# A hybrid pooling, convolution and mixture-of-experts step: later state loads, a sample tile held in quarters, gathered rows used block by block, two added products

## The reference

```python
mod = silu(c) @ w_ada + b_ada              # 6 parts of 1024, a row per sequence
h = rmsnorm(x, norm1) * (1 + sc1) + sh1
u, gate_b, gate_c, val = split(h @ w_in)   # 4 x 512
pool_out, pool_state = pool_mixer(u, prefix, ...)      # trailing means over 2, 4, 8, 16 tokens
conv_out, conv_state = conv_mixer(gate_b, gate_c, val, ...)  # three taps over C*h
x = x + g1 * (concat([pool_out, conv_out]) @ w_out)
h2 = rmsnorm(x, norm2) * (1 + sc2) + sh2
logits = h2 @ w_router + b_router          # 32 experts, the best 4 of each token
x = x + g2 * moe(h2)                       # clamped SwiGLU, softmax over the 4 logits
y = rmsnorm(x, final_norm)
```

## Time and profile before

| | |
|---|---|
| median of 3 runs | 1306.57 us (1305.33 to 1307.25) |
| profiled execution, its own time | 1306.41 us |
| its span | 1304.6 us |
| PE busy | 1255.8 us, 96% of the span |
| DVE, ACT, POOL busy | 525.5, 90.9, 230.4 us |
| data moved | 487.32 MB, 374 GB/s over the span |
| start of the input projection | 41.84 us |
| start of the first expert's products | 278.74 us |
| idle time of PE from 290 us to the end of the experts | under 1 us |

### The profile page before, as it was taken

One profiled execution on the slowest core, in us unless ns is written; L12 is line 12 of the kernel. 1 busy time (PEld: TensorE's weight loads), 2 busy tenths in 40 slices (PEclk: granted clock), 3 DMA queues, 4 the chain that ended last, 5 costly groups with the idle time before them and its releaser, 6 DMA issues.

```text
span 1304.6 us, 32026 instructions
## 1 busy us (share of the span) xinstructions
PE 1255.8 (96%) x14083; PEld 578.7 (44%) x14083; DVE 525.5 (40%) x823; ACT 90.9 (7%) x166; POOL 230.4 (18%) x296
## 2 busy tenths in 40 slices
PE   3999999869999999999999999999999999999997
PEld 2687764523444444333333333333444444433344
DVE  1222313556444444444333333333444444444356
ACT  3210011210000000000000000000000000000002
POOL 5001200030111111122222211121111111112100
PEclk9899999969999999999999999999999999999999
DMA  9877762268999999999999999999999999999994
GB/s 323 278 278 279 274 261 94 104 260 347 408 424 424 426 426 425 425 426 420 421 427 424 423 429 416 425 426 424 425 423 417 427 428 424 427 427 425 423 422 156
DMA packets 63430, 487.32 MB, mean 374 GB/s; under 512 B 11191, under 2 KB 20759, under 8 KB 38053
## 3 DMA queue, kind: packets, MB, share of 16 engines
q1 hardware_dynamic: 47442, 455.92, 84.3%
q0 software_dynamic: 10592, 19.87, 4.2%
q10 hardware_dynamic: 5363, 11.05, 2.3%
HBM read 468.22 MB, written 25.88 MB: 379 GB/s over the span
## 4 chain that ended last, share of the span: by engine, by line
PE 93%; DVE 3%; DMA 2%; issue 1%; ACT 1%; SPq 0%; POOL 0%; DVEq 0%; POOLq 0%
PE acc L1943 51%; PE acc L1968 24%; PE acc L943 9%; PE acc L987 4%; DMA raw<-in_w_ada 2%; PE acc L860 1%; PE acc L2050 1%; PE acc L878 1%; PE acc L998 1%; ACT h_t L486 0%; PE acc L2066 0%; DVE picked L1624 0%; PE acc L959 0%; PE acc L983 0%; POOL rows L1412 0%
## 5 line engine op out<-in xcount | busy, mean ns | idle before, releaser
L1943 PE MATMUL acc<-raw_b,ht 128*32 128x512 f32 x3024 | 332.9, 596 | 5.7 <-DVE ht L1578 5.7
L1943 PE MATMUL acc<-raw,ht 128*32 128x512 f32 x2928 | 319.8, 592 | 0.0
L1681 DVE TENSOR_TENSOR g_sb<-acc,bias_gu 128x768 f32<-128x768 f32 x32 | 30.7, 958 | 521.9 <-PE acc L1943 521.9
L1412 POOL DMA_INDIRECT rows<-h_rows,row_next x90 | 92.7, 1030 | 701.3 <-DVE row_next L1573 654.1
L1943 PEld LDWEIGHTS acc<-raw_b,ht 128*32 128x32 f32 x3024 | 98.3, 111 | 234.7 <-issue 228.2
L1943 PEld LDWEIGHTS acc<-raw,ht 128*32 128x32 f32 x2928 | 95.1, 110 | 205.7 <-issue 200.4
L1968 PE MATMUL acc<-raw,at 128*32 128x256 f32 x2976 | 166.3, 379 | 0.0
L1968 PE MATMUL acc<-raw_b,at 128*32 128x256 f32 x2976 | 166.3, 379 | 0.0
L1968 PEld LDWEIGHTS acc<-raw_b,at 128*32 128x32 f32 x2976 | 96.7, 110 | 77.1 <-issue 18.5
L1968 PEld LDWEIGHTS acc<-raw,at 128*32 128x32 f32 x2976 | 96.7, 110 | 63.9
L943 PE MATMUL acc<-h_t,raw 128*128 128x288 f32 (+1 forms) x512 | 120.1, 397 | 1.1 <-DVE h_t L700 1.1
(11 more groups left out here) (257 smaller groups left out, 646.4 us busy)
## 6 DMA issues: line engine op xcount, KB each, us to landing
raw<-in_w_down SPq DMA_DIRECT2D x33, 2048.0 KB, 12.0
raw<-in_w_gate SPq DMA_DIRECT2D x31, 2048.0 KB, 9.1
raw<-in_w_up SPq DMA_DIRECT2D x31, 2048.0 KB, 13.4
raw_b<-in_w_gate SPq DMA_DIRECT2D x31, 2048.0 KB, 9.8
raw_b<-in_w_up SPq DMA_DIRECT2D x31, 2048.0 KB
raw_b<-in_w_down SPq DMA_DIRECT2D x31, 2048.0 KB
raw<-in_w_ada SPq DMA_DIRECT2D x24, 1024.0 KB, 11.7
expert_rows<-zeros ACTq DMA_DIRECT2D x1, 8704.0 KB, 30.6
```

What stands on the lines that cost most here:

```text
L1412: pool.indirect_dma_start(rows[:, b, :], None, h2_quarter, bass.IndirectOffsetOnAxis(ap=idx[:, b:b + 1], axis=0), bounds_check=Q * NTOK - ...
L1681: dve.tensor_tensor(g_sb[:, :, :], gate_of(i, 0), plus(0), ALU.add).then_inc(g_read, 1)
L1943: mm = pe.matmul(gu_of(i)[b][q * TB:(q + 1) * TB, :].rearrange("p (m n) -> p m n", m=2), ht_of(i)[:, b, k, :], w[:, kk, :, q * CW:(q + 1) ...
```

## The change

- **State loads.** In the opening ACT loads the bias rows of the parts sh1 and sc1 only. The loads of parameters and states, the bias rows of the other four parts, and four new loads of the sample rows (`x_q`) come after the modulation of `h_t`, ahead of the loads of L556 to L562. PE turns parameters and states between `project(2)` and `project(3)`; ACT copies them out (`empty_states`) after `leave(3)`, ahead of the issue of the zero fill and of `leave(4)`. DVE's pooling windows wait for that copy, as they did.
- **Sample tile in quarters.** `x_q` and `h_q` hold the sample rows as 4 x 32 partitions x 256 columns. A product with a constant `same_s` (built by POOL in five steps) adds the four partial sums of squares. The tile is turned by 2 transposes, not 8. ACT stores it as four transfers of 32 KB, and later copies `x_q` into `x_sb` for the final sum. The g1, shift and scale rows of the sample tile are read back as four transfers each, not one, on POOL's queue.
- **Order on PE.** The prompt state's transposes move behind the turning of tile 3 and write another PSUM pair; the sample states' transposes move behind the ranks and write `tp`; the g2 products wait until ACT has copied them out (`so_ready`, 4).
- **Rows block by block.** Expert 0's three gathers have a semaphore each. `turn_first` turns block after block, and `gate_up_first` multiplies each block by the first half of the weights' rows as it comes; the rest goes as before. The turning now stands ahead of the softmax sums on DVE. SP waits for the same three semaphores.
- **Two products** (`keep_clock`) of 128 x 512 on weights in slot 0 stand ahead of expert 0. Nothing reads their result.

```diff
+            ada_bias(SH1, SC1 + 1, rows_loaded)
             act.wait_ge(tp_full, TP["c"] + 1)
             act.activation(c_sg[:, :, :], c_ps, ACT.Sigmoid).then_inc(tp_free, 1)
             norm_row(n1_rows, norm1, rows_loaded)
-            act.dma_start(par_rows[0:GR, :], pool_scale[0].rearrange("(g p) -> g p", p=P)).then_inc(state_loaded, 16)
...
+            act.dma_start(sc_rows, state_conv[0].rearrange("b r d -> (b r) d")).then_inc(state_loaded, 16)
+            ada_bias(G1, PARTS, n2_loaded)
+            for q in range(Q):
+                act.dma_start(x_q[q * NS:(q + 1) * NS, :],
+                              x_sample.rearrange("b t d -> (b t) d")[:, q * QW:(q + 1) * QW]).then_inc(xq_loaded, 16)
             act.dma_start(wpool_sb[:, :, :], w_pool[0].rearrange("g c d -> c g d")).then_inc(small_loaded, 16)
...
             for g in range(GR):
                 leave(g, uext[:, g, PAST:PAST + SEQ], uext_s[:, g, :, PAST:PAST + DEC_T])
+                if g == GR - 1:
+                    empty_states()
...
+            dve.wait_ge(mix_done, TT)
+            dve.wait_ge(xq_loaded, 16 * Q)
+            step(dve.tensor_tensor(h_q[:, :], mixp[PT % 2][:, 0, 0:QW], g1_q[:, :], ALU.mult))
+            dve.tensor_tensor(x_q[:, :], x_q[:, :], h_q[:, :], ALU.add).then_inc(x1_ready, 1)
+            dve.wait_ge(x1_ready, TT)
+            step(dve.tensor_tensor(h_q[:, :], x_q[:, :], a2_q[0][:, :], ALU.mult))
+            best(PT - 2)
+            dve.wait_ge(sq_done, TT + 1)
+            step(dve.reciprocal(rstd_q[:, :], rstd_q[:, :]))
+            dve.scalar_tensor_tensor(out=h_q[:, :], in0=h_q[:, :], scalar=rstd_q[:, 0:1], in1=a2_q[1][:, :],
+                                     op0=ALU.mult, op1=ALU.add).then_inc(h_ready, 1)
...
-            for k in range(4):
+            for k in range(3):
                 project(k)
+            pe.wait_ge(state_loaded, 16 * 4)
+            take("par")
...
+            pe.matmul(ss_ps, same_s[:, :], ss_q[:, 0:1], start=True, stop=True).then_inc(ss_summed, 1)
+            router(3)
+            take("h4")
...
+                def turn_first():
+                    for b in range(SB):
+                        dve.wait_ge(first_gathered[b], 16)
+                        ins = dve.transpose(ht[:, b, :, :], rows[:, b, :].rearrange("p (i k) -> p k i", k=KT))
+                        ins.then_inc(first_turned, 1)
...
+                def keep_clock():
+
+                    pe.wait_ge(slot_loaded[0], loaded_value(0, 0))
+                    for n in range(2):
+                        pe.matmul(psum[:, 1, :], slots(0)[:, n * P:(n + 1) * P], slots(0)[:, HALF:2 * HALF],
+                                  start=True, stop=True)
...
+                pe.wait_ge(so_ready, 4)
...
-                gate_up(0)
+                keep_clock()
+                gate_up_first()
```

More of the change, by code:

```diff
@@ new lines, in _ @@
+            act.wait_ge(h_ready, TT + PT + 1)
+            for q in range(Q):
+                act.dma_start(h2_dram[SEQ:NTOK, q * QW:(q + 1) * QW], h_q[q * NS:(q + 1) * NS, :])\
+                    .then_inc(h2_stored[PT % 2], 16)
+            act.wait_ge(so0_full, 1)
+            states(0, acc_u)
+            for q in range(Q):
+                act.activation(x_sb[0:NS, PT, q * QW:(q + 1) * QW], x_q[q * NS:(q + 1) * NS, :], ACT.Copy)\
+                    .then_inc(xs_rows, 1)
+            act.wait_ge(so_full, 1)
```

242 lines of the change are left out of this document (134 added, 108 removed).

## The result

The changed kernel takes 1312.26 us (median of 6 runs, 1311.15 to 1313.25) beside 1306.86 us for the kernel before (6 runs, 1304.03 to 1307.34). The ratio is 1.0045, 95% interval 1.0032 to 1.0058. It is slower by 0.45%; 1302.5 was forecast. The profiled execution took 1311.15 us, with a span of 1309.4 us; before it was 1304.6.

The account below looks back on a forecast made before the run. PE, holding 93% of the chain of waits, was taken as the bound. Opening and projection +4.55 us (-2.4 - 1.95 + 3.6 + 1.5 + 3.8) and tail -8.6 gave -4.05: 1306.57 to 1302.5 us, range 1297.5 to 1307.5.

Parts of the forecast that it names:

- opening: traffic and transposes: Before the projection: less load traffic gains 2.4 us, and state transposes moved off PE's way gain 1.95 us.
- block 2 waits for ACT: First projection blocks: twelve added issues delay ACT's first copy, so block 2 waits; +3.6 us, bounds 1.7 and 5.6.
- lower clock in blocks 6 and 7: Projection after the parameters and states: a lower clock there only raised that term's upper bound, 4.8 instead of 3.8 us.
- tail, up to the end of the first expert's gate and up products: From mix(4): first expert starts 6.2 us earlier, regained clock gives 2.4; together -8.6 us, between -5.5 and -10.
- twelve take 5.8 us: ACT's queue ahead of its first projection copy: twelve added issues at 0.485 us each take 5.8 us.
- the stall of the `br_bc` issue grows with what lies ahead of it: ACT's queue in the projection: the 4.61 us stall grows by 2 us; used only for block 2's upper bound, 5.6.
- a first expert that starts d earlier should end the run d earlier: Expert loop: weights are there in time and PE hardly waits, so an earlier first expert shortens the run equally.
- the weights of the second expert are late: Expert loop: one of three listed signs that would show the prediction wrong; no size given.
- The slower one: Projection: ACT's issue queue fills, block 2 starts 26 us behind the projection's start; projection part +11.6, time 1309.6; chance 0.08.
- The one on the stores: Ahead of the gathers: last quarter store lands at 268 or later, gain 5.5 instead of 8.6, time 1305.6; chance 0.15.
- The rival that the clock does not come back: First expert: despite the two products the clock returns no earlier, 2.8 us lost as before, time 1304.9; chance 0.10.
- The fastest one, small stalls: Projection: short issues, clock stays up, traffic gain 3.5; projection part about 0, time 1298; chance 0.22.

Follow-up runs that it names:

- e12: e10 without the two products ahead of the first expert; 1297.80 us, ratio 0.9949 to the kernel before.
- e1: Changed kernel with opening and projection as before the change, only its tail (from mix(4) on) kept; 1302.29 us, ratio 0.9972 to the kernel before.
- e4: Changed kernel without the two products (`keep_clock`) ahead of the first expert; 1310.55 us, ratio 1.0038 to the kernel before.
- e6: Changed kernel, but SP issues the later slots' expert weights only after the four quarter stores have landed; 1313.19 us, ratio 1.0060 to the kernel before.
- e8: Changed kernel with the first expert's rows turned in one step when all three blocks have landed; 1313.19 us, ratio 1.0056 to the kernel before.
- e10: Changed kernel with the edits of e9, e3 and e7 together; 1296.25 us, ratio 0.9927 to the kernel before.
- e9: Changed kernel with all ACT issues but the four state loads moved behind the copies of the first two blocks; 1303.71 us, ratio 0.9984 to the kernel before.
- e5: Changed kernel plus unused 128 x 512 products, five ahead of block 2 and two ahead of block 6; 1305.57 us, ratio 0.9996 to the kernel before.
- e3: Changed kernel with ACT copying block 4 before parameters and states, not after; 1308.13 us, ratio 1.0020 to the kernel before.
- e7: Changed kernel, but weights of expert 1's second part are issued only when expert 1's rows have landed; 1307.87 us, ratio 1.0018 to the kernel before.
- e11: e1 with e7's wait for expert 1's rows ahead of the second part's weights; 1299.32 us, ratio 0.9953 to the kernel before.
- e2: Changed kernel with eight of twelve added ACT issues (bias parts, sample rows) moved behind block 3's copy; 1304.11 us, ratio 0.9988 to the kernel before.

## Why the prediction was wrong

Its sum is -4.05 us; the profile shows +4.8 in the span. Term by term, from the rows of the two profiles:

| term of the sum | forecast, us | measured, us |
|---|---|---|
| opening: traffic and transposes | -4.35 | -4.39 |
| block 2 waits for ACT | +3.6 | +4.70 |
| lower clock in blocks 2 to 5 | +1.5 | +1.77 |
| parameters and states | +3.8 | +3.78 |
| lower clock in blocks 6 and 7 | 0 (bound +1.0) | +3.09 |
| tail, up to the end of the first expert's gate and up products | -8.6 | -8.8 |
| expert 1's rows, and the clock after them | none | +4.2 |
| the rest of the run | 0 | +0.4 |

**Right.** The opening, the two stands and the tail were each there, with the right releasers. The opening's total hides a split: the traffic gave 1.8 us, not 2.4, the transposes 2.0, and 0.6 came from a shorter last chunk and its turning, which the sum did not have. It is also a lucky pair of profiles, since the projection starts at 36.3 to 38.4 us in the eleven profiles with this front and at 41.7 to 43.1 in the three with the old one, 5.0 us apart on average. mix(4) begins 0.9 us earlier against the end of the projection (forecast 0.87), the ranks 4.63 (4.45), the first expert 6.1 (6.2), and the clock gives 2.7 (2.4). That the ranks fit so well is luck in part: with the same code this stretch took 2.1 us less to 1.7 us more in other profiles (e12, e1 to e4, e6, e8 to e10). One of these is right by two errors: the stores landed 2.2 us later than taken, but then DVE's operation of 2.16 us ended 0.16 us after the first gather had begun, and the gather took 1.13 us instead of being held. (The steps to the ranks add up to 261.1 us, not 261.3.)

**Mis-sized: block 2.** The step "twelve take 5.8 us" was too high (4.7 us from 36.77 to 41.5). The step that failed is the one kept for the upper bound alone, that the stall of the `br_bc` issue grows with what lies ahead of it: 8.09 for 4.61 us, 3.5 us more. The issues behind it then took 1.4 us less than before, so ACT's first copy came 6.8 us later against the projection's start, not 5.8. e9 showed that the stand goes when the issues stand elsewhere; whether the queue's content or the busy DMA engines make the issue long stays open. As the forecast value stood, the stall was a constant, although the text itself said that it looked like a full queue.

**Failed: the clock after the second stand.** The sum took it as 0 and put it into the upper bound. It took 3.1 us, and e5 and e3 showed that it is the clock. The price itself was read from the wrong place: the clock before the first expert had fallen 16 us before the stand to which the prediction put it down. The Trainium skill, "TensorE: Matmul & The Clock Gate", section HAM oscillation, says that bursts parted by waits lose the clock again each time. Three stands in the changed kernel agree (1.77, 3.09 and 1.7 us lost behind 4.83, 2.36 and 2.49 us); the one of 1.04 us before the first expert cost nothing. "Each time" is not borne out by e9, where 2.36 us at the same place cost nothing. The prediction weighed the rule for block 2 only. With the measured 3.1 us for the second stand its sum would have been -1.0 us.

**Missed: the wait for expert 1's rows.** The step "a first expert that starts d earlier should end the run d earlier", read from the waits of SP and from PE's lack of idle time, was false. No idle time says that nothing is late, and not by how much. The slack was 3.9 us, and the terms of the tail, the block-wise turning and the regained clock, used it up. The prediction named "the weights of the second expert are late" as what would make it wrong; it was the rows. e7 showed that the weights were early, and in the rows' way.

**The rivals.** The slower one had its mechanism right in kind and wrong in size: block 2 began 21.4 us behind the start, not 26. The time came out slower because three medium losses met, 1.1, 3.1 and 4.2 us. The one on the stores nearly had its premise come true (268 or later): 267.2 against the forecast's 265 with the projection's loss taken off, at no cost. That rival matters for e6: the Trainium skill, "DMA: Bandwidth & Descriptors", section Bandwidth, would give an estimated 3.8 us for four small stores, one after the other, by its table. The runs show 8.1 us beside weights and at most 2.8 without, so what lies beside them made 5 us of difference. What their size does was not tested: the single store of 128 KB landed 5.7 us after its issue, also beside 4 MB of weights, but issued later behind them. The rival that the clock does not come back fell: with the two products it is back 1.2 us before the expert starts, and without them (e4) the first 96 records take 1.46 us more. The fastest one, small stalls, fell with block 2's stand of 4.83 us.

## What to carry to other kernels

Before adding issues to a queue whose engine also has copies to make, ask what the queue and the DMA engines have to do at that point: the same issue took 1.6 us when they had been idle and 8 to 9 us behind state loads and beside weight loads, and a matrix engine two steps away stood still. "Nobody waits here" is not a number: before moving a start, follow the next consumer's chain too and write down its slack, because an edit that starts a stage earlier, or clocks it higher, takes from it. And price a stand of the matrix engine twice, its length and then the clock after it (0 to 3.3 us here), and where it can't be closed, fill it with products. Before you read 1 or 2 us out of a single profile, look whether the granted clock fell in a stage that the edit does not touch.

## What the runs showed of the hardware

- An issue on ACT's queue: `br_bc`, 16 KB, took 1.6 us in e9, e10 and e12, where the DMA engines had been idle; 3.30, 4.61 and 6.19 us in e11, the kernel before and e1; and 8.09 to 9.16 us in the changed kernel and e2 to e8. Four loads more ahead of it (e2) made it as long as twelve. Queue and traffic were not separated.
- The clock behind a stand: kept after 1.43 us (e5), lost for about 1.7 us after 2.47, 2.49, 2.54 and 2.59 us (e1, changed, e2, e3). After the same 2.36 us at the states it cost 3.1 us in the changed kernel, 3.3 in e7, 1.9 in e4, e6 and e8, 1.7 in e2 (17.75, 17.94, 16.59 and 16.40 us for 14.7) and nothing in e9 (14.91, against 14.93 in e3 without the stand). Ahead of the first expert 2.37 us cost 0.1 us in e5 (10.65 us for 10.51), and 2.38 us cost 1.5 in e9 (12.06). What tells these apart stays open.
- The clock without a long stand: in mix(4) it stayed up in five profiles (before, changed, e7, e11, e12: 1.93 or 1.94 us for the first 32 records) and fell in nine (2.93 to 3.47 us), all behind the same wait of 1.11 us.
- Rows of expert 1 landed 4.7 to 4.9 us after the start of the last gather with its second part's weights held back (e7, e10 to e12), 5.2 with them issued 1.2 us behind the gather (e6), and 7.2 to 8.7 in the other nine profiles, with 2 or 4 MB issued between 1.9 us ahead of it and 0.9 behind. Within these the amount does not order them: 8.65 us with 2 MB (e8), 7.26 with 4 MB (e5).
